# A four-mixer trunk on one core: the last adding DMAs behind the loads of v, and the turned y one step later

## The reference, cut to what matters

```
def spatial_gating_layer(x, norm_g, w_in, v_norm_g, w_s, b_s, w_out):   # layer A
    h = rms_norm(x, norm_g)
    u, v, z = jnp.split(h @ w_in, 3, axis=-1)      # 512 x 2048 @ 2048 x 12288
    u = jax.nn.gelu(u)
    v = rms_norm(jax.nn.gelu(v), v_norm_g)
    v = v.reshape(b, n_chunks, CHUNK, A_GROUPS, A_GROUP_DIM)
    mixed = jnp.einsum('gts,bcsgd->bctgd', w_causal, v) + b_s.T[None, None, :, :, None]
    y = u * mixed * jax.nn.silu(z)                 # 512 x 4096
    return y @ w_out                               # 4096 x 2048
x = x + spatial_gating_layer(...); x = x + forgetting_attention_layer(...)   # layer B
```

## Time and profile before

| what | us |
|---|---|
| median of 3 runs (lowest, highest) | 2277.71 (2274.69, 2279.99) |
| the profiled execution's own time | 2281.32 |
| its span | 2279.6 |
| outside of the span | 1.7 |
| PE busy | 2235.8 (98%) |
| DVE busy | 1706.1 (75%) |
| ACT busy | 1094.1 (48%) |
| POOL busy | 220.1 (10%) |

### The profile page before, as it was taken

One profiled execution on the slowest core, in us unless ns is written; L12 is line 12 of the kernel. 1 busy time (PEld: TensorE's weight loads), 2 busy tenths in 40 slices (PEclk: granted clock), 3 DMA queues, 4 the chain that ended last, 5 costly groups with the idle time before them and its releaser, 6 DMA issues.

```text
span 2279.6 us, 26439 instructions
## 1 busy us (share of the span) xinstructions
PE 2235.8 (98%) x10261; PEld 1829.0 (80%) x10261; DVE 1706.1 (75%) x1753; ACT 1094.1 (48%) x1319; POOL 220.1 (10%) x290
## 2 busy tenths in 40 slices
PE   7999999999999999999999999999999999999999
PEld 6788888888888888888778878877778878788887
DVE  8878877877877777898653387976977877677665
ACT  6745545454554454555342455444454454443432
POOL 0011001001211200001000000110110110121000
PEclk9999999999999999999999999999999999999999
DMA  8678777778988976898774455686686687764323
GB/s 286 226 251 279 239 258 239 243 267 254 289 259 259 278 238 217 275 294 271 245 224 157 132 173 174 202 269 194 199 286 215 203 292 246 262 217 143 99 88 120
DMA packets 252668, 516.41 MB, mean 227 GB/s; under 512 B 21488, under 2 KB 37408, under 8 KB 251520
## 3 DMA queue, kind: packets, MB, share of 16 engines
q1 hardware_dynamic: 198800, 383.31, 53.1%
q0 software_dynamic: 28304, 85.25, 12.1%
q10 hardware_dynamic: 25440, 46.17, 5.4%
HBM read 423.39 MB, written 103.97 MB: 231 GB/s over the span
## 4 chain that ended last, share of the span: by engine, by line
PE 70%; DVE 12%; issue 7%; DMA 7%; ACT 2%; POOL 1%; SPq 0%; ACTq 0%; DVEq 0%; POOLq 0%
PE ps L1403 16%; PE ps L1405 16%; PE ps L1404 16%; DVE u_lo L1876 5%; DVE raw L1847 3%; DMA yf_rows<-yf_rows 3%; PE ps L1582 3%; PE ps L1584 3%; PE ps L1583 3%; PE ps L1796 3%; PE ps L1798 3%; PE ps L1797 2%; DMA raw<-in_b_w_in_dram 2%; ACT u_hi L890 2%; PE ps L1712 2%
## 5 line engine op out<-in xcount | busy, mean ns | idle before, releaser
L890 ACT ACTIVATE u_hi<-raw 128x1536 fp32r<-128x1536 f32 (+1 forms) x332 | 560.9, 1690 | 768.7 <-PE ps L1405 691.5
L1876 DVE TENSOR_TENSOR u_lo<-raw,u_hi 128x1536 fp32r<-128x1536 f32 (+1 forms) x332 | 666.5, 2007 | 278.0 <-ACT u_hi L890 277.1
L1403 PE MATMUL ps<-u_hi,x1h 128*128 128x512 f32 x1408 | 557.8, 396 | 24.3 <-DVE u_lo L1876 16.7
L1404 PE MATMUL ps<-u_lo,x1h 128*128 128x512 f32 x1408 | 549.4, 390 | 0.0
L1405 PE MATMUL ps<-u_hi,x1l 128*128 128x512 f32 x1408 | 548.9, 390 | 0.0
L1403 PE MATMUL ps<-u_hi,x2h 128*128 128x512 f32 x1056 | 418.9, 397 | 5.0 <-DVE u_lo L1876 4.1
L1405 PE MATMUL ps<-u_hi,x2l 128*128 128x512 f32 x1056 | 412.2, 390 | 0.0
L1404 PE MATMUL ps<-u_lo,x2h 128*128 128x512 f32 x1056 | 411.7, 390 | 0.0
L1403 PEld LDWEIGHTS ps<-u_hi,x1h 128*128 128x128 f32 x1408 | 264.6, 188 | 102.9 <-DVE u_lo L1876 35.8
L1405 PEld LDWEIGHTS ps<-u_hi,x1l 128*128 128x128 f32 x1408 | 264.7, 188 | 56.2
L1404 PEld LDWEIGHTS ps<-u_lo,x1h 128*128 128x128 f32 x1408 | 264.9, 188 | 52.3
(11 more groups left out here) (250 smaller groups left out, 2361.6 us busy)
## 6 DMA issues: line engine op xcount, KB each, us to landing
raw<-in_a_w_in_dram SPq DMA_DIRECT2D x280, 512.0 KB, 4.7
raw<-in_b_w_in_dram SPq DMA_DIRECT2D x184, 512.0 KB, 4.7
t_rows<-t ACTq DMA_DIRECT2D x176, 256.0 KB, 5.4
raw<-t_rows SPq DMA_DIRECT2D x176, 256.0 KB, 4.9
raw<-in_a_w_out_dram SPq DMA_DIRECT2D x48, 512.0 KB, 5.5
w_raw<-in_a_w_out_dram SPq DMA_DIRECT2D x64, 256.0 KB, 3.3
w_raw<-in_b_w_out_dram SPq DMA_DIRECT2D x64, 256.0 KB, 2.8
vz<-vz_rows POOLq DMA_DIRECT2D x16, 512.0 KB, 5.1
```

Of the source, the lines that this page charges most:

```text
L890: act.activation(u_hi[:, u_of(g), 0:n, :], raw_of(g)[:, 0:n, :], ACT.Copy).then_inc(hi1_ready, 1)
L1403: pe.matmul(dst[:, t, :], a, u_hi[:, s, pos, :], start=first, stop=False, skip_group_check=more)
L1404: pe.matmul(dst[:, t, :], a, u_lo[:, s, pos, :], start=False, stop=False, skip_group_check=more)
L1876: dve.tensor_tensor(u_lo[:, u_of(g), 0:n, :], raw_of(g)[:, 0:n, :], u_hi[:, u_of(g), 0:n, :].bitcast(F32), ALU.subtract).then_inc(lo1_read ...
```

## The change

Two things are moved, and nothing is added or taken away. On GpSimd's queue `forms(j - 1, 4)`, the last of the adding DMAs, goes behind the wait for `y0_ready` and the two loads of v, and ahead of the copy of x. On ACT and DVE the parts of turned y are made one step later each: parts 0 to 4 at steps 3 to 7 of the second half of block 13, parts 5 to 15 at tile steps 0 to 10. SP's program is the same.

```diff
@@ gpsimd
                 if 1 <= j <= 4:
                     for e in range(2):
                         pool.wait_ge(yA_stored[e], 16 * j)
-                    for n in range(5):
+                    for n in range(4):
                         forms(j - 1, n)
                 pool.wait_ge(y0_ready, j + 1)
                 for e, buf in enumerate((cA, eU)):
                     pool.dma_start(buf[:, :, :].rearrange("p s (c d) -> p (s c d)", d=GD),
                                    v_dram[2 * j + e, :, :, :].rearrange("p c d -> p (c d)")).then_inc(v_loaded[e], 16)
+                if 1 <= j <= 4:
+                    forms(j - 1, 4)
                 if j < NF:
@@ scalar, block 13
-                            if u == NS - 1 and k >= 2:
-                                y_high(k - 2)
+                            if u == NS - 1 and k >= 3:
+                                y_high(k - 3)
@@ scalar, tiles
-                    if f == 0 and k + 6 < KB:
-                        y_high(k + 6)
+                    if f == 0 and k + 5 < KB:
+                        y_high(k + 5)
@@ vector, block 13
-                    if u == NS - 1 and k >= 2:
-                        y_low(k - 2)
+                    if u == NS - 1 and k >= 3:
+                        y_low(k - 3)
@@ vector, tiles
                     if f == 0:
-                        if k + 6 < KB:
-                            y_low(k + 6)
+                        if k + 5 < KB:
+                            y_low(k + 5)
```

## The result

The changed kernel is slower. Its median is 2285.56 us (2281.63 to 2287.97, 10 runs) against 2280.09 (2274.69 to 2284.40, 10 runs) of the kernel before, whose median of 3 runs was 2277.71. The ratio is 1.0024, 95% interval 1.0015 to 1.0033, so +5.5 us (3.4 to 7.5). The forecast was +1.7 us and 2279, with 0.57 on no measurable difference; the measured time is 0.06 us above the top of the range.

The account below looks back on a forecast made before the run. PE, busy 98% of the span at full clock, was taken as the bound. The terms -2.3 - 3.6 + 7.6 = +1.7 us on the median of 2277.7 gave 2279 us, range 2272.5 to 2285.5.

Parts of the forecast that it names:

- Part 1: GpSimd's queue: loads of v go out 4.5 and 4.8 us earlier, ending PE's gaps at groups 1 and 4; gain 2.3 us.
- Part 2a: Block 13: the later part of y ends PE's 1.93 us stall ahead of step 5 and the low clock; gain 3.6 us.
- Part 2b: Tiles of f = 0: SP's weights wait for later parts of y, so tile 5 stalls and turns slow; cost 7.6 us.
- the tiles stay fed: Rival at the tiles: weights of tiles 5, 7, ... come in time, cost 1 us, so 2272.8 us; chance 0.2.
- The second rival: SP's wait ahead of each weight: two-tile turn as slow as the three-tile turn, +6.1 us, 2283.8; chance 0.2.
- The third: Rival: adding DMAs hold the load of v, or part 2 lands after 8 us; up to 3 us lost, 2282; chance 0.1.

Follow-up runs that it names:

- forms only: Changed kernel with the parts of turned y put back to their old steps, so only the move on GpSimd's queue against the kernel before; ratio 0.9998 (0.9990 to 1.0007).
- the second trace: The changed kernel run once more without a further edit; ratio 1.0022 (1.0013 to 1.0031) to the kernel before.

## Why the prediction was wrong

**Part 1, a gain of 2.3 us that isn't there.** The step that failed is the price of the stalls at the mixes. The wait on ACT was real (loads issued 4.5 us late) and the move takes it away, but PE loses only what ACT waits beyond 3.0 us, and the waits differ between executions: the four traces with the old queue lose 2.3, 0.2, 0 and 1.1 us, 0.9 in the mean. And the move doesn't make PE's idle less. Between 400 and 1090 us, where the groups are, the stalls over 0.25 us add up to 0 to 1.9 us in the four traces with the old queue (mean 0.9) and to 0.3 to 2.4 in the nine with a new one (mean 1.0). Whether the move itself brings the stalls that stand elsewhere isn't shown. My lower bound of 0 was right, my value was the upper bound, taken from one execution. The times say 0: old against new queue side by side differ by 0.0 +- 1.5 us, and forms only is 0.5 us faster by its ratio with an interval of +-2.

**Part 2a, direction right, size too large as far as can be told.** The stall ahead of step 5 is in all three traces with the old order (1.93, 2.09, 2.15 us), each time with the low clock behind it, and in none of the ten with the new one. The five measurements of kernels without slow tiles are 0.7 to 1.4 thousandths faster, 1.6 to 3.2 us, with a mean of 2.2, against 3.6 forecast; each interval alone (up to 4 or 5 us) doesn't exclude 3.6. A is 1158.8 us in the mean of the three old traces and 1153.3 in that of the ten new ones, 5.5 less, but most of that is the draw of the executions: the three old ones took 1.2, 4.5 and 4.0 us more than their kernel's median, nine of the new ones 0.3 less in the mean (the tenth has no median). An estimate from these leaves some 2 us. Why the stall and the low clock behind it are worth less than their 3.6 us stays open. The old traces have one low spell each elsewhere in the mean, the new ones 1.3 outside of the tiles (one of double length counted as two), too few to tell.

**Part 2b, right in mechanism and size.** Weight 5 was issued at +4.9 (forecast +4.4; before it was -1.33, where the forecast has -1.4), took 10.1 us (10.2), and tile 5 stalled 2.64 us (2.4). The turns were 7.7, 6.9, 6.5 and 5.7 us (7.0, 7.0, 7.0, 6). The last small stall stood ahead of tile 12, not 13. The first 192 matmuls took 52.0 us, forecast 51.2; the second trace has 50.8. The cost was 7.6 us in the forecast, 7 to 8.3 in B, 7.1 in the times.

**The rivals.** That the tiles stay fed was wrong in both traces. The second rival has nearly the right time (+6.1) for the wrong reason: it asked for turns of 8.3 us, and none was that long. The third, that gains stay away, came true for part 1 in its outcome, not by its reason: the loads of v were not held, there was little to gain. So the sum was off since a gain read off a single execution was taken at its full value, 2.3 us, and 3.6 us of part 2a stood for 2.2. With these two at what the runs show, the same working gives -0 - 2.2 + 7.6 = +5.4, but only in hindsight. That the time left the range as well is due to the reference: the median of 3 runs was 2.4 us below that of 10, and 2277.7 + 5.5 = 2283.2 lies inside.

The page DMA: Bandwidth & Descriptors of the Trainium skill (Anatomy of one DMA) gives its form for a single DMA issued by GpSimd. Carried over to three loads on SP's queue, it gave an estimate of 3.8 us from the issue of a part to the landing of the weight behind it. The trace disagrees: it has 1178.37 - 1172.62 = 5.8 us in the first full turn, and 4.9 and 4.5 in the next two, so all three are above the page's form.

## What to carry to other kernels

When a consumer of a load is moved one step later, look at the queue that waits for it, not at the consumer: here SP's queue held the next weight behind a wait for the part, and a lead of three tiles became two, less than one turn of load, split and release. A turn's time divided by the tiles that it spans, set against the pace of the bound engine, tells it before the run. And a stall of about a microsecond in one trace is not yet a gain: look for it in a second execution. Ask how long the wait behind it may get before the bound engine feels it (3.0 us at the mixes here), since a wait that ends near that limit shows as a stall in one execution and as nothing in the next.

## What the runs showed of the hardware that was not expected

The granted clock's low spells don't follow from the length of the stall alone. The stall ahead of step 5 of block 13 (1.93 to 2.15 us) was followed by one in 3 of 3 traces. The stall at 1094 us (1.64 to 2.21 us) is in every one of the 13 traces and was followed by one in 2. The stall at the start of layer B's steps (about 2.7 us, in all) met one in 4. Two stalls between 1587 and 1614 us (about 2.2 us, in all, and 1.0 to 2.6 us some 14 us later) together met one in 7 of 13, the most frequent place of all. Each spell is 3.4 us at half the clock, one of them twice that, which costs 1.7 us if nothing makes up for it (an estimate). Often a later gap makes up for it: in the four traces where a spell met the start of layer B's steps, the stall of 2.0 us some 6 us behind it is gone, and the nine others have it; in the four where one stood at the first of the last two stalls, the second is 1.0 to 1.1 us, and 2.5 in the nine others. Three traces had no spell at all. The two traces of the changed kernel have four and none, those of the kernel before one and three, with spans of 2279.6 and 2282.9 us: part of the spread between executions of the same program.
